# The first expert pair's rows by one-hot products from the residual, in place of a gather and transposes

## The reference, cut to what matters

```python
    t = h.reshape(B * S, C)                                # 512 x 1024, RMS-normed
    group = jnp.argmax(g_logits, axis=-1)                  # one group of 4
    e_sel = jnp.take_along_axis(e_logits, group[:, None, None], axis=1)[:, 0]
    top_val, top_idx = lax.top_k(e_sel, TOP_K)             # two experts of its 8
    ...
    for gi in range(G):
        hid = jax.nn.silu(jnp.einsum('td,edf->tef', t, w1[gi])) * jnp.einsum('td,edf->tef', t, w3[gi])
        hid = hid * gate[:, gi, :, None].astype(hid.dtype)
        y = y + jnp.einsum('tef,efd->td', hid, w2[gi]).astype(f32)
```

## Time and profile before

| | |
|---|---|
| median of 3 runs | 1840.77 us (1838.44 to 1843.23) |
| profiled execution, its own time | 1835.3 us |
| its span in the trace | 1833.6 us |
| TensorE busy | 1609.1 us, 88% |
| VectorE busy | 600.6 us, 33% |
| granted TensorE clock, mean over the span | 0.947 of full |

### The profile page before, as it was taken

One profiled execution on the slowest core, in us unless ns is written; L12 is line 12 of the kernel. 1 busy time (PEld: TensorE's weight loads), 2 busy tenths in 40 slices (PEclk: granted clock), 3 DMA queues, 4 the chain that ended last, 5 costly groups with the idle time before them and its releaser, 6 DMA issues.

```text
span 1833.6 us, 26659 instructions
## 1 busy us (share of the span) xinstructions
PE 1609.1 (88%) x11565; PEld 840.2 (46%) x11565; DVE 600.6 (33%) x1162; ACT 416.6 (23%) x823; POOL 168.6 (9%) x189
## 2 busy tenths in 40 slices
PE   4999989998899999969878589999999997988871
PEld 2444468887454454534323244445544545333330
DVE  5210766663561121434111131206410324421114
ACT  2103245553300221301000120007511303010001
POOL 2000122330000000011111200000000000111102
PEclk9999999999899999979989879999999997998996
DMA  6119000000541411369999542211015024799994
GB/s 231 46 46 315 0 3 4 4 4 3 206 163 67 184 46 55 120 249 414 423 425 423 231 185 92 92 46 47 1 54 221 0 96 194 304 423 425 425 410 168
DMA packets 82071, 313.87 MB, mean 171 GB/s; under 512 B 18088, under 2 KB 19168, under 8 KB 57184
## 3 DMA queue, kind: packets, MB, share of 16 engines
q1 hardware_dynamic: 69280, 282.76, 39.3%
q0 software_dynamic: 11520, 25.19, 3.7%
q10 hardware_dynamic: 1152, 4.19, 0.6%
HBM read 305.81 MB, written 35.39 MB: 186 GB/s over the span
## 4 chain that ended last, share of the span: by engine, by line
PE 71%; issue 7%; DVE 5%; ACT 3%; DMA 2%; POOL 1%; PEld 0%; DVEq 0%; SPq 0%; POOLq 0%; ACTq 0%
PE PS L2097 14%; PE PS L545 14%; PE PS L559 11%; PE PS L1013 7%; PE PS L2122 6%; PE PS L1351 5%; PE PS L1337 2%; PE PS L2082 2%; PE PS L1313 1%; PE PS L1548 1%; PE PS L1569 1%; PE PS L484 1%; PE PS L1559 1%; PE PS L1701 1%; PE PS L1146 1%
## 5 line engine op out<-in xcount | busy, mean ns | idle before, releaser
L545 PE MATMUL PS<-arena,ring 128*128 128x512 f32 (+1 forms) x1024 | 414.9, 567 | 0.0
L545 PEld LDWEIGHTS PS<-arena,ring 128*128 128x128 f32 x1024 | 195.0, 191 | 216.4 <-issue 211.1
L559 PE MATMUL PS<-ring,arena 128*128 128x512 f32 x448 | 194.0, 592 | 0.7 <-ACT arena L1514 0.7
L2097 PE MATMUL PS<-ring,arena 128*64 128x512 f32 x512 | 131.6, 673 | 49.8 <-issue 46.8
L2097 PE MATMUL PS<-arena 128*64 128x512 f32 x512 | 121.8, 631 | 16.4 <-issue 13.6
L559 PEld LDWEIGHTS PS<-ring,arena 128*128 128x128 f32 x448 | 84.6, 190 | 104.3 <-issue 103.3
L1351 PE MATMUL PS<-ring,arena 128*128 128x512 f32 x256 | 113.6, 595 | 0.0
L2097 PEld LDWEIGHTS PS<-ring,arena 128*64 128x64 f32 x512 | 44.0, 155 | 135.5 <-issue 132.1
L2105 DVE TENSOR_TENSOR arena<-PS,arena 128x256 f32<-128x256 f32 x32 | 13.6, 425 | 273.8 <-PE PS L2112 253.4
L573 ACT ACTIVATE arena<-PS 128x512 f32<-128x512 f32 (+1 forms) x56 | 31.7, 566 | 307.4 <-PE PS L545 307.4
L2102 ACT ACTIVATE arena<-PS 128x256 f32<-128x256 f32 x32 | 12.3, 384 | 366.1 <-PE PS L2097 366.1
(11 more groups left out here) (295 smaller groups left out, 1923.8 us busy)
## 6 DMA issues: line engine op xcount, KB each, us to landing
arena<-in_moe_w SPq DMA_DIRECT2D x96, 1024.0 KB, 8.2
ring<-in_moe_w SPq DMA_DIRECT2D x96, 1024.0 KB
ring<-in_sb_wqkv SPq DMA_DIRECT2D x6, 2048.0 KB, 8.1
ring<-in_xa_wkv SPq DMA_DIRECT2D x4, 2048.0 KB, 15.6
ring<-in_xa_wq SPq DMA_DIRECT2D x4, 2048.0 KB, 8.5
ring<-in_xa_wo SPq DMA_DIRECT2D x4, 2048.0 KB, 13.7
h<-in_x SPq DMA_DIRECT2D x8, 512.0 KB, 5.2
ring<-in_rw_wr SPq DMA_DIRECT2D x2, 2048.0 KB, 13.2
```

The source lines that it names most:

```text
L545: ins = pe.matmul(PS[:, g % NBANK, 0:n], ring[:, u % RING, k, P * (j % 4):P * (j % 4) + P], xt[:, k, 0:n], start=(k == 0), stop=(k == KC - 1))
L559: ins = pe.matmul(PS[:, g % NBANK, :], xt[:, k, P * t:P * t + P], ring[:, (u0 + half) % RING, k, :], start=(k == 0), stop=(k == KC - 1))
L2097: ins = pe.matmul(bank(2, 2, F)[r, :, :], xgT[p][:, k, r], w[a][:, :, k, :], start=(k == 0), stop=(k == KC - 1))
```

## The change

The rows of pair 0 no longer come over HBM. In `place(t)` VectorE makes four further operations a tile: `first_w`, the two weights of a token (its RMS factor where its first or second expert lies in pair 0, and zero elsewhere), two one-hot matrices token by slot that carry these weights (`first_k`), and their sum `first_of`. TensorE multiplies the columns of the residual by it (`first_rows(t)`, 8 products of 128 columns a tile, summed over the four tiles), which gives at once, in banks 0 and 1, what `turn(0)` gave: the 128 slots' rows, normed and transposed. The gather of pair 0 and `turn(0)` are gone. The counts of `onehots` are renumbered, and `xg_free` is released right behind the last part of the table.

```diff
         def moe_route_pe(pe, l):
             def filled_table(t):
-                pe.wait_ge(S("onehots"), 28 * l + 3 * (t + 1))
+                pe.wait_ge(S("onehots"), 32 * l + (5, 9, 12, 15)[t])
...
+            def first_rows(t):
+                pe.wait_ge(S("onehots"), 32 * l + (5, 9, 12, 16)[t])
+                for k in range(KC):
+                    ins = pe.matmul(bank(k // 4, 4, P)[:, k % 4, :], h[:, t, k::KC], first_of[:, t, :],
+                                    start=(t == 0 and k % 4 == 0), stop=(t == NT - 1 and k % 4 == 3))
+                return ins
+
             for t in range(NT - 1):
                 filled_table(t)
+            first_rows(0)
             route_ranks(pe, l, NT - 1)
+            first_rows(1)
+            first_rows(2)
             filled_table(NT - 1).then_inc(S("tabled"), 1)
+            for p in range(2):
+                pe.nop().then_inc(S(f"xg_free{p}"), 1)
+            first_rows(NT - 1).then_inc(S("xg_free0"), 1)
             pe.wait_ge(S("chosen"), 2 * NT * (l + 1))
             scores_read(pe, l, 8)
             pe.matmul(PS[:, 4, 384:384 + NE], ones[:, :], cum[:, NT, :], start=True, stop=True).then_inc(S("ranked"), 1)
...
+                w = first_w[:, :]
+                do(vec.tensor_scalar(w, OB[:, t, :, 0], rstd[:, t:t + 1], None, ALU.mult))
+                for k in range(2):
+                    m = NT * k + t
+                    ins = vec.tensor_scalar(first_k[:, k, :], iob, s8[:, m:m + 1], w[:, k:k + 1], ALU.is_equal, ALU.mult)
+                do(ins)
+                vec.tensor_tensor(first_of[:, t, :], first_k[:, 0, :], first_k[:, 1, :], ALU.add)\
+                    .then_inc(S("onehots"), 1)
+
...
-            for n in range(4):
+            for n in range(1, 4):
                 fetch(n)
...
-            pe.wait_ge(S("table_ready"), l + 1)
-            for p in range(2):
-                pe.nop().then_inc(S(f"xg_free{p}"), 1)
-            turn(0)
             for n in range(NPE):
                 up_pair(n)
```

More of the change, by code:

```diff
@@ L1626, in trunk @@
         more_ = at(33.625, [256])
+        first_of = at(33.125, [NT, P])
+        first_k = at(23.75, [2, P])
         OSo = at(26, [4, P])
@@ L1653, in trunk @@
         ffn_eps = sb("ffn_eps", [P, 1])
+        first_w = sb("first_w", [P, 2])
         half_sq = sb("half_sq", [P, 1])
@@ L1739, in over_table_pe @@
             for m in range(8):
-                pe.wait_ge(S("onehots"), 28 * l + 12 + 2 * (m + 1))
+                pe.wait_ge(S("onehots"), 32 * l + 16 + 2 * (m + 1))
                 pe.matmul(PS[:, 5, NPE:2 * NPE], OSo[:, m % 4, :], OBo[:, m % 4, :], start=(m == 0), stop=(m == 7))\
@@ L1878, in moe_route_vec @@
                 .then_inc(S("table_ready"), 1)
-            no_row = wide_[:, 0:NPE]
+            no_row = more_[:, 0:NPE]
             do(vec.tensor_scalar(no_row, PS[:, 5, 0:NPE], 0.0, float(NBLK * BLK), ALU.is_ge, ALU.mult))
@@ L2135, in turn @@
             def turn(n):
-                pe.wait_ge(S(f"xg_in{n % 2}"), 16 * (NPE // 2 * l + n // 2 + 1))
+                pe.wait_ge(S(f"xg_in{n % 2}"), 16 * ((NPE // 2 - 1) * l + n // 2 if n % 2 == 0 else
+                                                    NPE // 2 * l + n // 2 + 1))
                 turn_rows(pe, n % 2, P).then_inc(S(f"xg_free{n % 2}"), 1)
```

## The result

| | before | after |
|---|---|---|
| median of 12 runs each, us | 1841.36 | 1846.63 |
| lowest and highest, us | 1838.44, 1845.87 | 1842.33, 1853.6 |
| ratio after to before, 95% interval | | 1.0027 [1.0016, 1.0039] |
| profiled execution, us | 1835.3 | 1844.97 |

The kernel became slower, by 0.27% or some 5 us (2.9 to 7.2 by the interval). I had forecast a gain of 10.9 us.

What follows compares the result with a forecast made beforehand. The experts' weight stream, begun by the end of `up` of pair 0, was taken to bound each MoE stage. Gains of 6.1 and 4.8 us in the two layers gave 1840.8 - 10.9 = 1829.9 us, range 1824 to 1839.

Steps and rivals of the forecast that it cites:

- the price of a `first_rows` record: TensorE's new products before `up` of pair 0: 0.214 us a record at low clock, 0.112 at full, mean 0.145.
- A product costs more than its rows say (slower): Rival, chance 0.05: the stationary operand's step of 8 makes products dearer; with p = 0.30, 1849.7 us.
- p = 0.230: Mean time in us of a `first_rows` record at which both layers together come out even.
- the recorded formula: End of `up` of pair 0 in layer 0 is 793.4 + 64p us, p being the mean `first_rows` record time.
- the clock: TensorE's clock rises to full at 788.3 us, during `first_rows(1)`, so `up` of pair 0 takes 7.09 us, not 9.47.
- VectorE: Four further operations in each `place` add 1.08 us (bounds 1.0 and 1.5), exposed in `place(1)`: tile 3's logits start at 777.44.
- ranks queued behind `first_rows(0)`: On TensorE, the last tile's ranks wait 1.46 us behind the first new products, 2.54 us later than before in all.
- one to one: Whatever moves the end of `up` of pair 0 moves the end of the whole MoE stage by as much.
- The later load of pair 2: The 4 MB load waiting for the last rows moves from 781.74 to about 783.9 us and costs nothing.
- gather of pair 1: Now the first gather, starting at 793.5 and landing at 801.0 us under `up` of pair 0, not delaying the weights.
- the sum: Both layers' earlier ends of `up` of pair 0, 6.1 + 4.8 = 10.9 us gained, giving 1829.9 us.

Runs made afterwards that it cites:

- experiment 1: Changed kernel, but the `first_rows` products read 128 neighbouring columns of `h`, not every eighth (values not the reference's): 1829.19 us, 0.9936 of before.
- experiment 5: Changed kernel with ScalarE writing normed rows column-regrouped, products and transposes reading them contiguously, `first_w` dropped, reference values kept: 1830.69 us, 0.993 of before.
- experiment 6: The kernel of experiment 5 with the last tile's ranks issued ahead of `first_rows(0)`: 1833.48 us, 0.9952 of before.
- experiment 7: Changed kernel with columns split so the products' slices have a step of 2, w1 and w3 loaded in 2 KB pieces: 1851.68 us, 1.0058 of before.
- experiment 4: Kernel before plus only VectorE's four further operations a tile, results unread, gather and transposes kept: 1840.41 us, 0.9999 of before.
- experiment 3: Changed kernel with only two products left in tile 0 and two in tile 3, VectorE's operations kept: 1826.9 us, 0.9925 of before.
- experiment 2: Changed kernel with the products' operand read at steps of 1, 8, 2 and 4 in tiles 0 to 3: 1840.94 us, single run.

## Why the prediction was wrong, step by step

**Failed: the price of a `first_rows` record.** I took "0.214 low and 0.112 full" from the table's products and from products at full clock, which read contiguous operands, and from transposes with the same step of 8. None was a product with a step, and I let two near rows stand for their combination. It runs at 0.239 at either clock, 0.243 with its pauses. The mechanism stood in the text as a rival ("A product costs more than its rows say (slower)", a chance of 0.05) with its point of decision, p = 0.230, and that held. Put p = 0.243 into the recorded formula: 793.4 + 64 x 0.243 = 809.0 instead of 808.83, and in layer 1, 762.05 us later, 1571.0 instead of 1569.51. That is 1.7 us lost in place of 10.9 won. The argument that I used against the rival, that transposes with this step keep their pace, is true and proves nothing for products. Its figure of 0.197 us was slightly off, as the last of those eight records takes 0.230 us and not 0.19: they come 0.192 apart on the mean, and 0.213 from the third on. Nothing in the sum used it.

**Half right: the clock.** With contiguous columns (experiment 1) it rose at 793.0 us, 10.6 behind the start of tile 3's logits, where I had forecast 788.3 - 777.44 = 10.9. With the step of 8 it rose at 796.2, 14.1 behind, and the rate of the records does not hang on it. Layer 0 of experiment 1 flatters the forecast, since the rise varies from stage to stage: 9.0 to 12.2 us behind in the eight stages of experiments 1, 5, 6 and 7, and 9.1 to 15.7 in the six of the changed kernel, five of them 14 or more. What I had not considered at all is that it could fall again before `up` did its work: 8.78 - 7.09 = 1.7 us more in layer 0. With that, the formula gives 3.4 us of loss, and the table of lengths shows 3.2. That they lie so close is in part luck: by layer the formula has 1.9 and 1.5 where the table has 1.3 and 2.0, and it takes the clock of one profile, while the six stages together lost 1.7 us to it in layer 0 each time and in layer 1 once in three. The measured 5.0 [2.9, 7.2] holds this; whether the other 1.7 us are anything but the spread of the stages stays open.

**Right: VectorE.** First the read of tile 1's ranks in the kernel before, which goes with the one at 776.09 in the earlier trace rows. Then the timeline of the changed kernel, VectorE (the reads of two tiles' ranks, with the new operations between, and the last tile's choice of experts):

```profile
775.07 0.21 DVE L1841 TENSOR_TENSOR arena<-arena,PS 128x64 f32<-128x64 f32 x1
```

```profile
779.77 0.21 DVE L1857 TENSOR_TENSOR arena<-arena,PS 128x64 f32<-128x64 f32 x1
781.90 0.21 DVE L1857 TENSOR_TENSOR arena<-arena,PS 128x64 f32<-128x64 f32 x1
...
789.67 0.19 DVE L1850 TENSOR_TENSOR arena<-arena 128x32 f32<-128x32 f32 x1
...
792.70 0.22 DVE L1857 TENSOR_TENSOR arena<-arena,PS 128x64 f32<-128x64 f32 x1 [2.73 <-PE PS L1722]
```

The two reads are 2.13 us apart, and 776.09 - 775.07 = 1.02 before: 1.11 more, where I had 1.08. The exposed part costs about 1.1 us a layer (experiment 4).

**Right: ranks queued behind `first_rows(0)`.** I had 1.46 us. The choice of experts ended at 789.86 and the ranks' load began at 791.58, 1.7 later; 16 records at 0.239 and not 0.214 make 0.4 us more. By experiment 6's profile it is the better order all the same.

**Right: one to one.** That the end of the stage follows the end of `up` of pair 0 is borne out within the spread of the stages. Experiments 1, 3, 5 and 6 gain 12.1, 15.1, 12.4 and 9.0 us at `up`, and by the medians 12.2, 14.5, 9.6 and 6.9 in the time. Experiment 7 gains 10.1 at `up` and loses only behind it, where the stream is slower. The later load of pair 2 and the gather of pair 1 cost nothing that shows.

**Right for the wrong kernel: the sum.** With the price of contiguous records the recorded sum of 10.9 us is what experiments 1 and 5 measure (by the medians 12.2 and 9.6 us, by the intervals of the ratios 8.1 to 15.5 and 8.6 to 17.1). From tile 3's logits to the end of `up` I had 802.70 - 777.44 = 25.26 us, and experiment 1 has 807.71 - 782.43 = 25.28.

## What to carry to other kernels

A price is taken from a row that has the same operation, the same operand role and the same stride. Where there is none, the combination is a cost of its own and gets both ends and a fair chance, above all when the break-even (here 0.230 against 0.214 at half clock) lies close. When work is moved to TensorE, look at how the stationary operand lies: if it is strided by four floats or more, let an engine with slack regroup it as it writes, as ScalarE does here at no cost that shows. And products ahead of a long stretch have a second worth in the clock at which that stretch starts.

## What the runs showed of the hardware that was not expected

- A float32 product with a strided stationary operand pays in a jump between a step of 2 and one of 4: 0.112, 0.120, 0.232 and 0.239 us a record for steps of 1, 2, 4 and 8 at full clock. With a step of 8 it takes 0.239 at half clock as well. A transpose of the same shape with a step of 8 keeps the pace of a contiguous one (0.110), though its load shows as 0.19 us and not 0.14.
- The clock did worse with products so slowed. In four of six stages with the step of 8, and in both of experiment 2, the granted clock was at 0.50 for some of `up`'s first microseconds, though it had been at 1.00 during the products ahead of it; this happened in none of eight stages with a step of 1 or 2. `up` of 32 records took 8.6 to 8.8 us and not 7.1. TensorE's pause just ahead of `up` is the same in both (in layer 0 1.72 us in the changed kernel, 1.71 in experiment 1), so it isn't that alone. What in the slowed products does it, or whether it is the time at which they run, no run here tells.
- w1 and w3 in pieces of 2 KB in place of 8 KB: 407 against 424 GB/s in the middle of the stage, with the DMA engines' mean busy share at 1.04 and 1.01, and some 8 us a stage.
